# POOL's low halves in four instructions of 256 columns, its Hyena sums in two

## What is computed

```python
hn = rmsnorm(x, norm1_w);  proj = hn @ w_in                        # 2048 x 11280
conv_out = centred_depthwise_conv(proj[..., :SHORT_CONV_CH], conv_w, conv_b)
kf = two_sided_spectrum(hyena_filters(...))                        # rfft of 512
z   = hx1 * long_conv(hv, kf[:, 0], hb[0])                         # irfft(rfft(u) * kf) + u * bias
y_a = hx2 * long_conv(z, kf[:, 1], hb[1])
y_b = o * (mlstm_direction(q, k, v, ...) + flip(mlstm_direction(flip(q), ...)))
x = x + (gate_a * (y_a @ w_branch_a) + gate_b * (y_b @ w_branch_b)) @ w_out
gu = rmsnorm(x, norm2_w) @ w_gate_up                               # 2048 x 11264
x = x + (silu(gu[..., :5632]) * gu[..., 5632:]) @ w_down
# the second block: a gated linear attention and a sparse attention side by side,
# then a feed-forward layer of the same size
```

## Time and profile before

| | |
|---|---|
| median of 3 runs (lowest to highest) | 2641.33 us (2639.22 to 2641.79) |
| the profiled execution, its own time | 2639.56 us |
| its span | 2637.7 us |
| PE busy | 2605.5 us (99%) |
| weight loads of PE busy | 2154.6 us (82%) |
| ACT / POOL / DVE busy | 1402.6 / 1195.8 / 1101.4 us |
| granted clock of TensorE, mean | 0.996 |
| read from HBM | 487.14 MB, 185 GB/s |

### The profile page before, as it was taken

The page is one execution under the profiler, slowest core; times in us unless marked ns, Lnnn a source line. Parts: engine busy times, 40 slices in busy tenths (PEclk is TensorE's granted clock), DMA queues, the critical chain, the costliest instruction groups (busy, mean ns, idle before and its releaser), DMA issues.

```text
span 2637.7 us, 30178 instructions
## 1 busy us (share of the span) xinstructions
PE 2605.5 (99%) x11888; PEld 2154.6 (82%) x11888; DVE 1101.4 (42%) x1314; ACT 1402.6 (53%) x1717; POOL 1195.8 (45%) x528
## 2 busy tenths in 40 slices
PE   9999999999999999999999999999999999999999
PEld 7878888788888888888888878878888888888887
DVE  5776854434342232323333566456432222222222
ACT  7666645445465555555544565555555555555333
POOL 2667653344444444444444455333444444444443
PEclk9999999999999999999999999999999999999999
DMA  8666554466566766666666544453556666666654
GB/s 294 206 185 184 171 192 166 155 220 209 198 207 201 208 206 207 207 207 199 207 213 205 204 144 160 147 205 128 176 192 207 207 200 207 202 209 205 203 202 144
DMA packets 166140, 513.74 MB, mean 195 GB/s; under 512 B 99579, under 2 KB 102620, under 8 KB 108656
## 3 DMA queue, kind: packets, MB, share of 16 engines
q1 hardware_dynamic: 165568, 511.30, 60.4%
q10 hardware_dynamic: 432, 0.52, 0.1%
HBM read 487.14 MB, written 2.10 MB: 185 GB/s over the span
## 4 chain that ended last, share of the span: by engine, by line
PE 89%; DVE 4%; ACT 2%; POOL 1%; issue 1%; DMA 1%; SPq 0%; ACTq 0%; DVEq 0%; POOLq 0%
PE PB L718 28%; PE PB L722 28%; PE PB L719 28%; ACT WH L1243 1%; POOL WL L2895 1%; DMA RAW<-in_w_in_a 1%; DVE WL L1969 1%; PE PB L797 1%; PE PB L959 1%; PE PB L736 0%; PE PB L922 0%; PE PB L834 0%; PE PB L844 0%; DVE VY L2753 0%; PE PB L906 0%
## 5 line engine op out<-in xcount | busy, mean ns | idle before, releaser
L2895 POOL TENSOR_TENSOR WL<-RAW,WH 128x1024 fp32r<-128x1024 f32 x441 | 1077.4, 2443 | 1423.4 <-ACT WH L1243 1423.3
L1243 ACT ACTIVATE WH<-RAW 128x1024 fp32r<-128x1024 f32 x889 | 938.7, 1058 | 1106.2 <-PE PB L722 1087.6
L1969 DVE TENSOR_TENSOR WL<-RAW,WH 128x1024 fp32r<-128x1024 f32 x448 | 609.3, 1361 | 1438.8 <-ACT WH L1243 1438.7
L718 PE MATMUL PB<-WH,HNH 128*128 128x512 f32 x2464 | 971.8, 394 | 5.4 <-ACT TM L1564 2.4
L722 PE MATMUL PB<-WL,HNH 128*128 128x512 f32 x2464 | 963.1, 391 | 8.2 <-POOL WL L2895 4.4
L719 PE MATMUL PB<-WH,HNL 128*128 128x512 f32 x2464 | 960.8, 390 | 0.0
L722 PEld LDWEIGHTS PB<-WL,HNH 128*128 128x128 f32 x2464 | 463.6, 188 | 110.1 <-POOL WL L2895 7.4
L718 PEld LDWEIGHTS PB<-WH,HNH 128*128 128x128 f32 x2464 | 463.9, 188 | 105.6 <-issue 6.2
L719 PEld LDWEIGHTS PB<-WH,HNL 128*128 128x128 f32 x2464 | 464.1, 188 | 94.9
L718 PE MATMUL PB<-WH,HDH 128*128 128x512 f32 x704 | 273.9, 389 | 0.0
L719 PE MATMUL PB<-WH,HDL 128*128 128x512 f32 x704 | 273.9, 389 | 0.0
(11 more groups left out here) (376 smaller groups left out, 1905.6 us busy)
## 6 DMA issues: line engine op xcount, KB each, us to landing
RAW<-in_w_gu SPq DMA_DIRECT2D x176, 1024.0 KB, 4.8
RAW<-in_w_dn SPq DMA_DIRECT2D x88, 1024.0 KB, 4.8
RAW<-in_w_in_a SPq DMA_DIRECT2D x53, 1024.0 KB, 4.8
RAW<-in_w_in SPq DMA_DIRECT2D x45, 1024.0 KB, 4.8
RAW<-in_w_out SPq DMA_DIRECT2D x32, 1024.0 KB, 4.8
RAW<-in_w_ga SPq DMA_DIRECT2D x24, 1024.0 KB, 4.8
RAW<-in_w_gb SPq DMA_DIRECT2D x24, 1024.0 KB, 4.8
WIN<-in_win SPq DMA_DIRECT2D x8, 512.0 KB, 5.8
```

What stands on the lines that cost most here:

```text
L718: e.matmul(o, hi[:, k, x], WH[:, s, c], start=k == 0, stop=False)
L1243: e.activation(WH[:, u % NSPL, :], RAW[:, n % NRAW, half * SU * 128:(half + 1) * SU * 128], ACT.Copy).then_inc(*wt.act.mark(("wh", u)))
L1969: e.tensor_tensor(WL[:, u % NSPL, :], RAW[:, n % NRAW, half * SU * 128:(half + 1) * SU * 128], f32(WH[:, u % NSPL, :]), ALU.subtract).then ...
L2895: e.tensor_tensor(WL[:, u % NSPL, :], RAW[:, n % NRAW, half * SU * 128:(half + 1) * SU * 128], f32(WH[:, u % NSPL, :]), ALU.subtract).then ...
```

## The change

Every subtraction RAW - WH of POOL becomes four instructions of 256 columns, one behind the other, of which only the last signals `wl`. The sums KS and UP of the Hyena stage, each one instruction of 512 columns, become two of 256. The HSD sums stay as they are, and so do DVE's and ACT's instructions. The wait in front of the first piece is the one there was; no semaphore is added. Every piece counts up POOL's semaphore by one, and the steps that others wait for are marked at the last piece, as before.

```diff
                 n, half = divmod(u, 2)
                 e.wait_ge(*wt.act.done("wh", u))
-                e.tensor_tensor(WL[:, u % NSPL, :], RAW[:, n % NRAW, half * SU * 128:(half + 1) * SU * 128],
-                                f32(WH[:, u % NSPL, :]), ALU.subtract).then_inc(*wt.pool.mark(("wl", u)))
+                for i in range(4):
+                    c, r = slice(256 * i, 256 * i + 256), half * SU * 128 + 256 * i
+                    e.tensor_tensor(WL[:, u % NSPL, c], RAW[:, n % NRAW, r:r + 256], f32(WH[:, u % NSPL, c]),
+                                    ALU.subtract).then_inc(*wt.pool.mark(*([("wl", u)] if i == 3 else [])))
...
-                    a, b = flat(KT[:, 0, :, :]), flat(KT[:, 1, :, :])
-                    e.tensor_tensor(flat(KS[:, 0, :, :]), a, b, ALU.add).then_inc(*hy.pool.mark())
-                    e.tensor_tensor(flat(KS[:, 1, :, :]), a, b, ALU.subtract).then_inc(*hy.pool.mark(("ks", blk)))
+                    for f, op in ((0, ALU.add), (1, ALU.subtract)):
+                        for ri in range(2):
+                            e.tensor_tensor(KS[:, f, ri, :], KT[:, 0, ri, :], KT[:, 1, ri, :], op).then_inc(
+                                *hy.pool.mark(*([("ks", blk)] if f and ri else [])))
...
-                    a, b = flat(Y[:, 0, :, :]), flat(Y[:, 1, :, :])
                     e.wait_ge(*hy.dve.done("y", blk, 1))
-                    e.tensor_tensor(flat(UP[:, 0, :, :]), a, b, ALU.add).then_inc(*hy.pool.mark())
-                    e.tensor_tensor(flat(UP[:, 1, :, :]), a, b, ALU.subtract).then_inc(*hy.pool.mark(("z", blk)))
+                    for f, op in ((0, ALU.add), (1, ALU.subtract)):
+                        for ri in range(2):
+                            e.tensor_tensor(UP[:, f, ri, :], Y[:, 0, ri, :], Y[:, 1, ri, :], op).then_inc(
+                                *hy.pool.mark(*([("z", blk)] if f and ri else [])))
```

## The result

The changed kernel takes 2652.32 us (median of 6 runs, 2645.99 to 2654.32) where the kernel before takes 2640.15 (6 runs): a ratio of 1.0044, interval 1.0033 to 1.0056. Measured again beside other kernels it stood at 1.0043 (1.0031 to 1.0055). That is 11 to 12 us slower, outside the range of 2632 to 2651 that was forecast, on the side and near the size of rival A. The profiled execution took 2651.53 us, its span is 2649.7: 12.0 us more than in the earlier trace rows.

A forecast was written before the change was run, and what follows sets the result against it. PE, busy 2605.5 of 2637.7 us, was taken as the bound; -9.2 - 3.5 + 8.1 + 1 + 3.8 = +0.2 us turned 2639.56 into 2639.8, expected median 2641, range 2632 to 2651.

The forecast's parts named there:

- rival A: Hyena blocks: each of seven may pay the full 2.2 us, plus clock falls (+3); +9.2 us, 2650; chance 0.28.
- Rival C: POOL runs its four pieces as one, DVE enters only after the fourth; +4 us, 2645; chance 0.08.
- part two: DVE operations behind POOL's halves wait at most 0.7 us instead of 2.4, shortening chains to PE's waits; -9.2 us.
- Rival B: Hyena stretch: DVE's shorter stands free PE banks and end POOL's chain sooner; -6.4 us, 2635; chance 0.22.
- the edges: Hyena stage: KS sums holding ScalarE, and longer PE stands bringing the lower clock; +1 us, between 0 and +4.
- part three: Hyena stage: longer POOL dispatches and extra DVE turns make halves late for PE across seven blocks; +8.1 us.
- the clamp's chain: Clamp at 43.97 us, feeding PE's wait on H of 1.4 us: all of it goes, -1.4 us.
- the scans: Scans at 1554.07 us and the product before them, ahead of PE's 3.7 us wait for DVE's WL; -2.5 us.
- (b): DVE's product M at 138.51 us, feeding the larger of PE's two waits on TM; -1.5 us.
- (d): Products TM x KN, the second standing behind a whole half: PE's wait of 0.9 us goes; -0.9 us.
- The clock term: Second layer, PE's waits before 1559.81 and 1837.13 us: shortened, most lower-clock loss goes; -3.5 us, ends 0 and -4.
- Part four: POOL's halves elsewhere, at 33, 1552.95, 1728, 1736, 1789 us and in the mLSTM stage, come later; +3.8 us together.

The follow-up runs named there:

- seven halves: Against the kernel before, only seven low halves of POOL behind which DVE stood were cut into pieces of 256, sums whole: 2634.86 us, ratio 0.9979.
- eight halves: Against the kernel before, eight chosen halves in four pieces, PE's first matmul with their WL waiting for only 512 columns: 2632.57 us, ratio 0.9974.
- halves only: Against the kernel before, all POOL halves WL in four pieces, the sums KS and UP whole: 2648.43 us, ratio 1.0030.
- whole, longer halves: Against the kernel before, each POOL half whole after a wait for its previous instruction, then three one-column fills, each behind a wait: 2646.18 us, ratio 1.0024.

## Why the prediction was wrong

**The mechanism stood.** Strict turns, DVE served sooner, POOL's late halves later, nothing in the feed-forward stretches, pieces of 0.8 us, POOL near 1400 us (1465), the wait for POOL WL over 10 us, those on X and on DVE's WL down to 4.2: all as listed. Rival C is out. In the second profile of the changed kernel and with seven halves the clamp starts 0.16 us behind POOL's first piece and takes 0.73 and 0.72 us, not 2.4. (In the first profile it takes 0.28, but there it starts ahead of the half and shows nothing.) So there is a seam between pieces of one tile too, and the rule of the Trainium skill that was weighed in part two (GPSIMD Engine Reference, section 2.1 Instruction dispatch) does not keep DVE out here. Rival B is out: PE's waits for POOL grew fivefold. Rival A came near the number, but not by its sum: it kept the -9.2 of part two whole and paid 18.4 us in the Hyena stage, where 10.4 and 11.6 were measured.

The terms can be set beside the stretches between the rows of the table. In brackets stand first how much longer PE stands, then how much longer it is busy (us):

| stretch, times of the kernel before | forecast | changed | changed again | seven halves |
|---|---|---|---|---|
| up to 62 | -1.0 | +2.7 (+2.2, +0.6) | -0.1 (+0.2, -0.3) | -0.3 (+0.7, -1.0) |
| 62 to 494 | +6.9, and +1 for the edges | +11.6 (+8.4, +3.3) | +10.4 (+7.5, +2.9) | -1.2 (-1.4, +0.3) |
| 1552 to 1857 | -3.2, and -3.5 for the clock | -2.3 (+0.9, -3.2) | +0.8 (-0.7, +1.5) | -3.3 (-3.1, -0.1) |

**Part two failed.** It said that a DVE operation "now waits at most 0.7 us in place of 2.4" and took that once for each chain. Nearly each operation of a chain pays a piece. The seven halves, which have part two but for the 0.9 us of the product before the scans, and hardly anything of part three, give -4.7 us in the profile and -4.9 in the medians where the sum had -9.2, and -12.7 with the clock. The missing part is where chains are longest: the clamp's chain -0.3 for -1.4, the scans -0.3 for -2.5 (the wait behind them -0.6). Nor does the product's 0.9 us help the chain: with eight halves it lasts as long, 7.2 us from the product's start to the end of DVE's WL, for 7.8 before. (b) came at -1.1 for -1.5, (d) at about -0.9, as forecast, the two waits on X together at -1.9 for -2.9.

**The clock term failed.** The -3.5 us left out that the changed kernel has new waits behind which the clock falls. In its first profile the clock does stay up at 1569 and 1851 us (1.00), and PE is busy 3.2 us less in the second layer; but it falls behind new waits at 38 us (0.57 from 38 to 42) and 260 us, and PE is busy 3.3 us longer in the Hyena stage. In the second profile it falls at the two places of the second layer again (0.57 from 1566 to 1570, 0.67 from 1848 to 1852), and nothing is gained. With seven halves PE still stands 3.1 and 2.1 us there, and the clock is as low as before:

```profile
1558.00:1563.00 5.00, 5.00 (x21) 4.62 (x21) 5.00 (x4) 2.34 (x2) 5.00 (x4) 0.50 0.64 210
1833.00:1837.00 4.00, 3.76 (x13) 3.10 (x14) 2.28 (x7) 2.17 (x8) 0.00 (x0) 0.57 0.54 227
```

**Part three held in kind, and its edges were too small.** +2.2 us per block was +1.8 in the block read above. Between 62 and 494 us the forecast of standing (8.1 + 0.3 - 1.5 for (b)) was +6.9; measured were +6.5 with halves only and +8.4 and +7.5 in the two profiles of the changed kernel. The +1 for the edges was for the lower clock too, and that alone took 3.3 and 2.9 us; with halves only it took nothing. The rest is the block near 283, taken as one without a DVE half queued (+0.9, swallowing a wait of 0.9): a DVE served sooner reached that point with its half. That is the argument that rival B's text had held against itself.

**Part four was mis-sized in two terms.** The first half, at 33 us, was put at +0.4. Its four pieces let DVE's half WL in (36.72, 1.25 us) and take some 3.8 us for 2.4, so +1.4. PE's wait there is 3.12 us in the first profile, where the clock fell and 1.6 us had been lost before, and 1.1 in the second, for 0.9. And the halves at 1728 and 1736 were +0.8 together: the waits behind them grow from 0.59 and 1.36 us to 0.99 and 2.77. From 1713 to 1836 the losses are +1.2, +2.6 and +5.5 us in three profiles with all halves in pieces, and +4.6 with whole, longer halves. The clock makes most of that spread: up to 1857 PE is busy 1.7 us less, 1.6 longer and 3.0 longer in the three, and stands 0.6, 0.3 and 1.9 us more. I had said that I counted the loads and had counted only the halves.

So 0.2 us became 11 to 12. By the table, the second layer came 4.4 and 7.5 us above its forecast, the Hyena stage 3.7 and 2.5, and the start 3.7 (of which 1.6 lie ahead of the change) and 0.9. How much of that the clock takes differs from profile to profile, and what decides whether it falls behind a wait stays open.

## What to carry to other kernels

Where two engines take turns on a resource by the instruction, cutting the instructions of one cuts the longest single wait of the other, not the wait of a chain: a chain of n operations can stand behind n pieces. And the one that is cut can lose a turn at every seam, which costs little where its result has slack and most where another engine already waits for it. So cut only the instructions behind which a late chain stands, keep those whole that are late themselves, and if something must be cut, let the consumer start on the first pieces: here 8 of 441 halves in pieces gave 6.7 us, and all 441 cost 8.6, or 12 with the sums.

## What the runs showed that I had not expected

The order at a seam is decided by tenths: an operation of DVE that comes 0.3 us sooner made POOL's half 1.3 us longer. Two profiles of the same changed kernel differ by 4 us at 494 us (+14.4 and +10.3), 2.8 of them already at 62, and end within 0.9 of each other, since the second layer then takes or gives. A stand of PE is not always followed by the lower clock: behind the wait of 2.77 us at 1569.10 in the first profile of the changed kernel the granted clock stays at 1.00, and behind that of 2.76 at 1565.03 in the second it is 0.57. A fill of one column holds POOL about 0.04 us when four of them follow one another (some 0.15 us together), and about 0.16 us behind a wait for the one before (0.5 us for three).
